# Three blocks of an expert stage: the second job's expert made fixed, 15 weight places instead of 12, 18 unrolled jobs instead of 8, and the gather of tokens cut in two

## The chip, the cores and the metric

The kernel runs on one NeuronCore of a Trainium2 chip. The metric is the device time of one execution in microseconds (us), taken as the median of several runs. The profile is one execution more; its times are counted from the start of its span.

## The reference, cut to what matters

Two models stand one behind the other, on 256 tokens of width 1024. The first (attention, gated feed-forward, a per-layer embedding; two layers) is untouched here. The second has two layers of a hybrid mixer (windowed attention beside a short convolution) and then this mixture of experts:

```
group  = argmax(x @ w_rg + b_rg)                  # 4 groups of 8 experts
e1, e2 = the two best of the group's 8 experts    # x @ w_re + b_re
y      = sum over e in (e1, e2) of gate_e * ((silu(x @ w_gate[e]) * (x @ w_up[e])) @ w_down[e])
```

There are 32 experts with matrices 1024x512, 1024x512 and 512x1024 in float32, so 2 MiB each and 6 MiB (6.29 MB) for an expert. The 256 tokens give 512 pairs of token and expert. On the fixed inputs the reference's routing gives every expert of the first layer at least one token (expert 0 has 16) and leaves one of the second layer empty, expert 21 (expert 0 has 9); no expert has more than 48.

## The kernel before, in words

**Jobs.** The expert stage (`moe(l)`, once for each of two layers) sorts the 512 pairs by expert into 512 slots. A job is one expert with a window of 64 slots (`W`). Expert e gets ceil(count/64) jobs, and each of the first `FORCED` = 10 experts at least one, even when it is empty. A small table `tab` holds the expert and first slot of each job and the number `more` of jobs that go through a hardware loop. Job 0 is always expert 0, so that its weights need no table. The table is made by a chain of small VectorE and TensorE instructions (`route`, lines 2433 to 2521, and lines 1703 to 1729) and copied out of PSUM on line 1073. The SyncE queue, which issues all weight loads, waits for it on line 698 before it reads the number of job 1's expert.

**Weights.** A job's weights are six halves of 1 MiB: gate 0, 1, up 0, 1, down 0, 1. There are twelve places of 1 MiB: six in `raw` and six in `spare`, a second name for the memory of `parts` (the rounded weights of the dense stages). In the first `FIXED` = 8 jobs, which are written out (unrolled), jobs 0, 2, 4 and 6 go to `spare` and the odd ones to `raw`. Later jobs use `raw` alone, in a hardware loop. Before a place is loaded again SyncE waits (line 658 to 672) until TensorE has counted its last use in the semaphore `used`. Loads are issued in one fixed order, two halves (2 MiB) at a time.

**Work of a job.** TensorE runs step j: turn the gate product of job j-1 (line 1788, 4 transposes), gate half 0 of job j (line 1779), turn the up product, gate half 1, turn the result of job j-2 (line 1798), up half 0 and 1, and the down product of job j-1 (line 1809). ScalarE and VectorE copy between them. The token window of a job, `xw`, is a copy that ScalarE makes out of `xsT`, the gathered and turned tokens (line 1091).

**Ahead of the jobs.** TensorE gathers all 512 slots by matmuls with a 0/1 matrix `sel` (128 x 512 for each half of the tokens): 8 column blocks x 2 token halves x 2 parts (high and low) = 32 matmuls of 128x512 on line 1742. Their stationary operand is `xsp`, read with a stride of 8 elements (`view(xsp[:, i, :], D * t + k, [[KC, P]])`). `sel` is written by VectorE on lines 2520 and 2521. ScalarE and VectorE scale the eight banks into `xsT` (lines 1079, 2540) and ScalarE copies job 0's window (line 1084). After job 0's four products TensorE turns `sel` for the later way back (line 1753) and sums the gates of each slot (line 1759), and only then step 1 begins. Short matmuls without use ("spin", line 1687) fill TensorE's waits during routing.

**After the jobs.** The results are turned back and added into the tokens (line 1870); in the first of the two layers the next layer's dense stage follows, whose loads stand behind the last job's in the SyncE queue.

Of the kernel before, what the change touches and what calls it, by code (L numbers as in the profile page):

```python
# [20 lines left out]
F32 = mybir.dt.float32  # L21
# [6 lines left out]
P = 128  # L28
# [22 lines left out]
JOBS = NE + NS // W  # L51
FIXED = 8
IN_PARTS = (0, 2, 4, 6)
FORCED = 10
# [11 lines left out]
C_ID, C_TRI, C_I512, C_I32, C_I4, C_VALID, C_COS, C_SIN, C_SEL, C_W = 0, 128, 256, 768, 800, 804, 805, 821, 837, 897  # L66
# [7 lines left out]
def build(nc, A, out):  # L74
    ctx = ExitStack()
    with ctx:
# [10 lines left out]
        h = sb("h", [P, NT, D])  # L87
        xT = sb("xT", [P, 2, KC, S], F32R)
# [128 lines left out]
        gsel = qkf[:, 2560:3584].rearrange("p (t s) -> p t s", t=NT)  # L217
        rt = qkf[:, 0:2048]
        gtmp = qkf[:, 2048:2560]
        asg0 = rt[:, 1280:1376]  # L220

        def gather_bank(k):

            return pb[(0, 1, 4, 5, 6, 7, 2, 3)[k]]
# [14 lines left out]
        arrived = [arrived[0], arrived[1], arrived[0], arrived[2]]  # L239
        hi_done = {g: sem(f"hi_done{g}") for g in (0, 2)}  # L240
# [56 lines left out]
        LOADS0 = []  # L297
# [50 lines left out]

        add_proj(0, A["w_in_ab"][0], [(512 * c, 512, 512 * c) for c in (0, 1, 3, 4, 2, 5)])
# [9 lines left out]
        for l in range(2):  # L359
# [10 lines left out]
            LOADS0.append(list(loads))  # L370
            for i in range(0, RAW, 2):
                loads[i] += len(IN_PARTS)

# [24 lines left out]
        def job_home(l, j, q):  # L398

            q -= q % 2  # L400
            if isinstance(j, int) and j <= FIXED:
                job, i = piece(j, q)
                if job in IN_PARTS:
                    part = (SPL0[2 * l + 1] + i // 2) % SPL
                    return spare[:, 2 * part:2 * part + 2, :], arrived[2 * l][i], 16 * (LOADS0[l][i] + job // 2 + 1)
                if job < FIXED - 1 or j < FIXED:
                    place = (RAW0[2 * l + 1] + i) % RAW
                    return raw[:, place:place + 2, :], arrived[2 * l + 1][place], 16 * ((job + 1) // 2)
            place = (RAW0[2 * l + 1] + q - 2) % RAW
            return raw[:, place:place + 2, :], arrived[2 * l + 1][place], at(j, 16, -8 * FIXED + (0 if q < 2 else 16))  # L410

        def last_half(l):

            return arrived[2 * l + 1][(RAW0[2 * l + 1] + 5) % RAW]

        def consumed(job, i):

            if job == 0 and i < 4:
                return (1, 3, 3, 4)[i]
# [2318 lines left out]
```

## Time and profile before

| what | us |
|---|---|
| median of 3 runs | 1922.22 |
| lowest and highest | 1920.95, 1923.99 |
| profiled execution, its own time | 1919.76 |
| its span | 1917.9 |
| TensorE busy | 1813.6 (95%) |
| VectorE busy | 862.6 (45%) |
| ScalarE busy | 763.7 (40%) |
| first expert stage: table's first load to last down product | 852.84 to 1323.4 |
| second expert stage, the same | 1445.04 to 1899.0 |

The mean granted TensorE clock of the execution is 0.991 of full speed. A busy TensorE is not one at its peak, since the ends of matmuls are modelled: two stages that both show it as busy can have different paces, which is read from the distance of like instructions. Most fp32 matmuls appear as two records, and some records are missing. The DMA share of a stretch is that of 16 engines, and may read slightly over 1.

### The profile page before, as it was taken

To read this page: it belongs to the slowest core of one execution; us is meant where nothing else is said; L and a number is where in the kernel's file an instruction comes from. 1 tells how busy PE (TensorE), PEld (TensorE's weight loads), DVE (VectorE), ACT (ScalarE), POOL (GpSimd) and SP (SyncE) were. 2 spreads that over 40 slices of the span, in tenths; PEclk is the share of its full clock that TensorE was granted. 3 is DMA by queue.
4 is the path that set the end of the run, shared out by engine and by line. 5 is a ranking of instruction groups with operands and counts; after the bars stand their busy time and mean duration, and the time that the engine had idled before them with its cause. 6 is when DMAs were issued, how large, how long until landed. Compare 5 with 4: busy or idle time off the path is not lost.

```text
span 1917.9 us, 27918 instructions
## 1 busy us (share of the span) xinstructions
PE 1813.6 (95%) x10239; PEld 1174.3 (61%) x10239; DVE 862.6 (45%) x1641; ACT 763.7 (40%) x1396; POOL 74.8 (4%) x98
## 2 busy tenths in 40 slices
PE   8999999998999999999999999999999999999997
PEld 6779998885799988874333333335975333333334
DVE  4766566578766566872211111114784111111113
ACT  5564334556543345523333332334532333333333
POOL 3300000110000000010000000000010000000000
PEclk9999999998999999999999999999999999999999
DMA  9546554551355545159999999998438999999995
GB/s 324 205 143 198 184 190 154 185 177 34 120 185 189 185 155 186 45 208 409 428 400 428 428 429 428 429 428 337 136 132 343 429 409 428 427 431 427 429 429 221
DMA packets 127696, 549.14 MB, mean 286 GB/s; under 512 B 7711, under 2 KB 67449, under 8 KB 103161
## 3 DMA queue, kind: packets, MB, share of 16 engines
q1 hardware_dynamic: 124200, 539.51, 71.4%
q0 software_dynamic: 3088, 8.10, 1.3%
q8 instruction: 59, 0.97, 0.2%
q10 hardware_dynamic: 320, 0.34, 0.1%
q14 instruction: 29, 0.23, 0.0%
HBM read 546.81 MB, written 1.11 MB: 286 GB/s over the span
## 4 chain that ended last, share of the span: by engine, by line
PE 65%; DMA 24%; DVE 6%; ACT 2%; issue 1%; POOL 1%; SPq 0%; POOLq 0%; DVEq 0%; ACTq 0%
PE pb L1242 27%; DMA raw<-in_w_expert_down 24%; PE pb L1809 12%; PE pb L1779 8%; PE pb L1537 6%; PE pb L1788 1%; PE pb L1371 1%; PE pb L1471 1%; PE pb L1798 1%; DVE parts L1963 1%; PE pb L1394 1%; PE pb L1348 1%; POOL rms L792 1%; PE pb L1742 1%; PE pb L1254 1%
## 5 line engine op out<-in xcount | busy, mean ns | idle before, releaser
L1779 PE MATMUL pb<-raw,xw 128*64 128x512 f32 x1760 | 415.0, 603 | 19.8 <-DMA raw<-in_w_expert_gate 19.7
L1963 DVE TENSOR_TENSOR parts<-raw,parts 128x2048 fp32r<-128x2048 f32 (+1 forms) x138 | 307.1, 2231 | 108.3 <-ACT parts L812 105.3
L812 ACT ACTIVATE parts<-raw 128x2048 fp32r<-128x2048 f32 (+1 forms) x138 | 256.6, 1867 | 209.7 <-PE pb L1242 153.2
L1242 PE MATMUL pb<-xT,parts 128*128 128x256 f32 (+1 forms) x2712 | 333.3, 283 | 0.0
L1242 PEld LDWEIGHTS pb<-xT,parts 128*128 128x128 f32 (+1 forms) x2712 | 329.2, 191 | 4.7 <-issue 2.9
L2555 DVE TENSOR_TENSOR qk<-qk,pb 128x256 f32<-128x256 f32 x126 | 53.1, 421 | 605.1 <-ACT qk L1101 605.0
L1242 PE MATMUL pb<-parts,xT 128*128 128x512 f32 (+1 forms) x1200 | 272.1, 385 | 2.9 <-DVE xT L1974 1.5
L1242 PEld LDWEIGHTS pb<-parts,xT 128*128 128x128 f32 x1200 | 217.9, 189 | 49.0 <-issue 4.3
L1779 PEld LDWEIGHTS pb<-raw,xw 128*64 128x64 f32 x1760 | 111.9, 136 | 204.2 <-issue 167.9
L1809 PE MATMUL pb<-raw,qk 128*64 128x512 f32 x880 | 201.0, 596 | 35.1 <-DMA raw<-in_w_expert_down 35.1
L1809 PEld LDWEIGHTS pb<-raw,qk 128*64 128x64 f32 x880 | 67.6, 136 | 162.9 <-issue 162.7
L1096 ACT ACTIVATE qk<-pb 128x512 f32<-128x512 f32 x126 | 74.9, 594 | 172.9 <-PE pb L1779 172.9
L1113 ACT ACTIVATE qk<-pb 128x512 f32<-128x512 f32 x126 | 68.4, 595 | 159.3 <-PE pb L1809 159.3
L1788 PEld LDWEIGHTS pb<-cst,qk 128*128 128x128 f32 x504 | 70.2, 209 | 98.5 <-issue 97.8
L1537 PE MATMUL pb<-parts,hidT 128*128 128x512 f32 x528 | 124.3, 391 | 3.1 <-DVE hidT L2197 3.1
L1537 PEld LDWEIGHTS pb<-parts,hidT 128*128 128x128 f32 x528 | 97.7, 188 | 23.3 <-DVE hidT L2197 3.9
L1101 ACT ACTIVATE qk<-pb 128x256 f32<-128x256 f32 x126 | 48.8, 388 | 146.4 <-PE pb L1788 146.2
L2573 DVE TENSOR_TENSOR work<-work,pb 128x256 f32 x126 | 53.0, 422 | 93.6 <-ACT work L1120 92.9
L1788 PE MATMUL pb<-cst,qk 128*128 128x128 f32 x504 | 93.7, 309 | 0.5 <-DVE rms L2583 0.5
L1120 ACT ACTIVATE work<-pb 128x256 f32 x126 | 48.4, 386 | 113.9 <-PE pb L1798 111.0
L1798 PEld LDWEIGHTS pb<-cst,qk 128*128 128x128 f32 x504 | 54.2, 141 | 48.1 <-issue 47.9
L1798 PE MATMUL pb<-cst,qk 128*128 128x128 f32 x504 | 68.6, 279 | 0.0
(322 smaller groups left out, 1490.3 us busy)
## 6 DMA issues: line engine op xcount, KB each, us to landing
raw<-in_w_expert_gate SPq DMA_DIRECT2D x55, 2048.0 KB, 10.0
raw<-in_w_expert_up SPq DMA_DIRECT2D x55, 2048.0 KB, 10.4
raw<-in_w_expert_down SPq DMA_DIRECT2D x53, 2048.0 KB, 10.7
raw<-in_w_ffn_gate SPq DMA_DIRECT2D x22, 1024.0 KB, 5.4
raw<-in_w_ffn_up SPq DMA_DIRECT2D x22, 1024.0 KB, 5.4
raw<-in_w_ffn_down SPq DMA_DIRECT2D x22, 1024.0 KB, 5.0
raw<-in_w_in SPq DMA_DIRECT2D x16, 1024.0 KB, 5.3
spare<-in_w_expert_gate SPq DMA_DIRECT2D x8, 2048.0 KB, 11.3
```

Source lines behind the costliest of these rows:

```text
L812: nc.scalar.activation(parts[:, (SPL0[seg] + k) % SPL, 0, 0:kk * nn], raw[:, place, 0:kk * nn], ACT.Copy).then_inc(hi_done[seg], 1)
L1096: nc.scalar.activation(dst, pb[bank][:], ACT.Copy).then_inc(done[l], 1)
L1113: nc.scalar.activation(ys[:, 512 * c:512 * (c + 1)], pb[4 + c][:], ACT.Copy).then_inc(ys_done[l], 1)
L1242: ins = mm(out_ap, b if flip else a, a if flip else b, start=first and n == 0, stop=last and n == 2)
L1537: ins = mm(pb[2 * c + t][:], hidT[:, j, i, P * t:P * (t + 1)], w[p][:, j, 512 * c:512 * (c + 1)], start=(q == 1 and j == 0 and n == 0), st ...
L1779: ins = mm(pb[m][rows, :], xw[:, 4 * hf + k, :], w[:, k, :], start=(hf == 0 and k < 2), stop=(hf == 1 and k >= 2))
L1788: ins = nc.tensor.transpose(pb[2 + m][:, P * q:P * (q + 1)], view(src, q, [[DE // P, P]]), ident)
L1798: ins = nc.tensor.transpose(pb[6 + b][:, P * q:P * (q + 1)], ys[:, 512 * b + P * q:512 * b + P * (q + 1)], ident)
L1809: ins = mm(pb[4 + c][W * k:W * (k + 1), :], ehj[:, 2 * hf + k, :], w[:, k, 512 * c:512 * (c + 1)], start=(hf == 0), stop=(hf == 1))
L1963: v.tensor_tensor(two[:, 1, :], raw[:, place, 0:kk * nn], two[:, 0, :].bitcast(F32), ALU.subtract)\
L2555: v.tensor_tensor(d, d, pb[2 + m][:].rearrange("p (k i s) -> p k i s", k=4, i=2)[:, :, 1, :], ALU.add)\
L2573: v.tensor_tensor(d, d, pb[6 + b][:].rearrange("p (k i s) -> p k i s", k=4, i=2)[:, :, 1, :], ALU.add)\
```

## The change

The 33rd bin takes what expert 0 has beyond 64 tokens, so that expert 0 always has exactly one job in front, and job 1 is always expert 1. Its weights are then loaded without the table. Three places of 1 MiB are added (`extra`, a second name for the memory of `xT` and `xs`, free once the router has read it). A planner (`plan`) hands out 15 places to the halves of jobs 0 to 18, singly where a pair would wait longer, and goes back to the six of `raw` for the last ones. `FIXED` goes from 8 to 18, `FORCED` from 10 to 20. The gather first makes 128 slots (`EARLY`) for jobs 0 and 1 in two banks, and the other 384 in two groups behind job 0's products and inside step 1. The turning of `sel` and the gate sums move into step 12 (`GATES_AT`). The first waits for the `raw` places are those of the last rounding of each place, not of all.

```diff
-JOBS = NE + NS // W
-FIXED = 8
-IN_PARTS = (0, 2, 4, 6)
-FORCED = 10
+BINS = NE + 1
+JOBS = BINS + NS // W
+FIXED = 18
+EXTRA = 3
+FORCED = FIXED + 2
+EARLY = 2 * W
+GATES_AT = 12
...
+        with nc.sbuf_tensor("extra", [P, EXTRA, HALF], F32) as extra:
+            pass
...
+        def first_wait(l, kind, i):
+
+            seg, n = 2 * l, len(stream[2 * l])
+            if kind == "raw":
+                before = max(k for k in range(n) if stream[seg][k][2] == (RAW0[seg + 1] + i) % RAW)
+                return [(lo_done[seg], before + 1)]
+            if kind == "spare":
+                return [(used[seg], n - SPL + i // 2 + 1)]
+            return [(rt_ready, l + 1), (sq_done, 2 * (7 + 2 * l) + 2)]
...
+            order = [(0, 0), (0, 2), (1, 0), (1, 2), (0, 4), (1, 4)]
+            for job in range(2, FIXED + 1):
+                order += [(job, 0), (job, 2)] + ([(job - 1, 4)] if job > 2 else [])
+            for job, i in order:
+                first = use_of(job, i)
+                if first >= LAST_FIXED - 6:
+                    put(job, i, [("raw", first % RAW), ("raw", first % RAW + 1)])
+                    continue
+                free = [p for p in places if p[0] != "raw" or first < LAST_FIXED - 12]
+                pair = min((p for p in pairs if p[0] in free), key=lambda p: max(rank[p[0]], rank[p[1]]))
+                single = sorted(free, key=lambda p: rank[p])[:2]
+                if max(rank[p] for p in pair) <= rank[single[1]] + (2 if job >= 7 else 0):
+                    put(job, i, pair)
+                else:
+                    put(job, i, single[:1])
+                    put(job, i + 1, single[1:])
...
@@ SyncE
-                sp.wait_ge(lo_done[2 * l], len(stream[2 * l]))
-                gate_up_of(0, 0)
-                down_of(1, 0)
+                units = PLAN[l][0]
+                early = [unit for unit in units if unit[0] < 2]
+                for unit in early:
+                    load_fixed(l, unit, unit[0])
                 sp.wait_ge(tab_done, l + 1)
...
@@ ScalarE
+                def gathered(half):
+
+                    for k in (4 * half, 4 * half + 2):
+                        act.wait_ge(ga_ready, (KC + 2) * l + 2 + k + 1)
+                        nc.scalar.activation(xsT[:, k, EARLY:NS], gather_bank(k)[:, 0:NS - EARLY], ACT.Copy,
+                                             scale=gperm[:, l, k:k + 1]).then_inc(xsT_a, 1)
...
@@ TensorE
-                spin(10)
+                mm(count, over, ones[0:1, :], start=True, stop=False)
+                mm(pos, ones[0:1, :], view(over, 0, [[0, 2], [1, BINS]]), start=True, stop=False)
+                pe.wait_ge(xsT_v, 9 * l + 1)
+                for b in (4, 5):
+                    mm(pb[b][:], ones[0:1, :], xsT[0:1, :, NS:NSP], start=True, stop=False)
+                spin(8)
...
-                spin(3)
-                pe.wait_ge(tab_done, l + 1)
+                for t in range(NT):
+                    for i in range(2):
...
+                        for k in range(KC):
+                            ins = mm(early_bank(k), tokens(i, t, k), sel[:, t, 0:EARLY],
+                                     start=False, stop=(t == 1 and i == 1 and k % 4 == 3))
...
+                def gathered(half):
+
+                    pe.wait_ge(sel_done, 6 * l + 4)
+                    for k in range(4 * half, 4 * half + 4):
...
+                        for t in range(NT):
+                            for i in range(2):
+                                ins = mm(gather_bank(k)[:, 0:NS - EARLY], tokens(i, t, k), sel[:, t, EARLY:NS],
                                          start=(t == 0 and i == 0), stop=(t == 1 and i == 1))
...
+                    if fixed == 1:
+                        gathered(1)
+                        pe.wait_ge(xsT_a, 4 * l + 3)
+                        pe.wait_ge(xsT_v, 9 * l + 8)
...
-                first = gate_up(0)
-                pe.wait_ge(xsT_a, 5 * l + 3)
-                products(0, *first[0])
-                products(0, *first[2], done=0)
-                pe.wait_ge(xw_ready[l], 1)
-                products(0, *first[1], done=2)
-                products(0, *first[3])
-                gates_turned()
-                pe.wait_ge(gct_done, 3 * l + 3)
+                for n, one in enumerate(gate_up(0)):
+                    if n < 2:
+                        pe.wait_ge(xsT_v, 9 * l + n + 2)
+                    products(0, *one)
+                gathered(0)
                 for j in range(1, FIXED):
                     step(j)
+                    if j == GATES_AT:
+                        gates_turned()
...
@@ VectorE
+                def chosen(t, cols):
+
+                    link(v.tensor_scalar(sel[:, t, cols], i512[:, cols], sl[0][:, t:t + 1], None, ALU.is_equal))
+                    v.scalar_tensor_tensor(sel[:, t, cols], i512[:, cols], sl[1][:, t:t + 1], sel[:, t, cols].bitcast(F32),
+                                           ALU.is_equal, ALU.add).then_inc(sel_done, 1)
...
+                for half in range(2):
+                    x, g = early(half)
+                    dve.wait_ge(ga_ready, (KC + 2) * l + half + 1)
+                    v.tensor_tensor(xw[:, 4 * half:4 * half + 4, :], x[:, :, 0:W], g[:, :, 0:W], ALU.mult).then_inc(xsT_v, 1)
```

## Rows read from the trace of the kernel before

**Rows 1.** The page: ScalarE's copies of gate and up products, two for each job.

```profile
L1096 ACT ACTIVATE qk<-pb 128x512 f32<-128x512 f32 x126 | 74.9, 594 | 172.9 <-PE pb L1779 172.9
```

**Rows 2.** The chain that ended last, end of the first expert stage (start, us, what).

```profile
978.28 10.92 DMA raw<-in_w_expert_down
989.33 3.67 PE pb L1809 x16
...
1297.70 3.65 PE pb L1809 x16
```

**Rows 3.** TensorE's timeline, first transposes of steps 2, 8 and 10, first stage.

```profile
886.10 0.75 PE L1788 MATMUL pb<-cst,qk 128*128 128x128 f32 x4
...
964.90 0.75 PE L1788 MATMUL pb<-cst,qk 128*128 128x128 f32 x4
...
992.92 0.75 PE L1788 MATMUL pb<-cst,qk 128*128 128x128 f32 x4
```

**Rows 4.** The same, steps 1, 2 and 10 of the second stage.

```profile
1464.15 0.75 PE L1788 MATMUL pb<-cst,qk 128*128 128x128 f32 x4 [0.25 <-DVE rms L2583]
...
1476.11 0.75 PE L1788 MATMUL pb<-cst,qk 128*128 128x128 f32 x4
...
1583.30 0.75 PE L1788 MATMUL pb<-cst,qk 128*128 128x128 f32 x4
```

**Rows 5.** Stretches: length; PE, PEld, DVE, ACT, POOL busy; clock; DMA share; GB/s.

```profile
900.00:920.00 20.00, 20.00 (x100) 8.06 (x102) 4.89 (x12) 7.19 (x17) 0.00 (x0) 1.00 1.01 428
...
966.00:980.00 14.00, 13.94 (x70) 5.43 (x68) 2.87 (x7) 4.92 (x12) 0.00 (x0) 1.00 0.87 325
```

**Rows 6.** SyncE's queue: the third early load, then the first load behind the table.

```profile
834.32 0.33 SPq L672 DMA_DIRECT2D spare<-in_w_expert_down  x1
852.84 0.35 SPq L672 DMA_DIRECT2D raw<-in_w_expert_gate  x1
```

**Rows 7.** VectorE's timeline: last op of the job columns; the longer one for `sel`.

```profile
850.30 0.25 DVE L2512 SCALAR_TENSOR_TENSOR qk<-cst,qk 32x40 f32<-32x40 f32 x1
...
851.62 0.75 DVE L2521 SCALAR_TENSOR_TENSOR hidT<-cst,qk,hidT 128x512 fp32r<-128x512 f32 x1
```

**Rows 8.** TensorE's timeline: job 0, turned `sel`, gate sums, step 1 (first stage).

```profile
862.48 7.09 PE L1779 MATMUL pb<-spare,xw 128*64 128x512 f32 x32
...
869.50 1.09 PE L1753 MATMUL pb<-cst,hidT 128*128 128x128 f32 x8
870.42 1.84 PE L1759 MATMUL pb<-ones,qk 128*128 128x1 f32 x16
872.52 0.98 PE L1788 MATMUL pb<-cst,qk 128*128 128x128 f32 x4 [0.26 <-DVE rms L2583]
```

**Rows 9.** The same of the second stage: gather, job 0.

```profile
1445.77 8.41 PE L1742 MATMUL pb<-hidT,xsp 128*128 128x512 f32 x32
1454.10 7.09 PE L1779 MATMUL pb<-spare,xw 128*64 128x512 f32 x32
```

**Rows 10.** Stretches of dense 256-column, dense 512-column and gather matmuls (columns as Rows 5).

```profile
776.00:780.00 4.00, 4.00 (x36) 4.00 (x35) 3.90 (x11) 1.79 (x9) 0.00 (x0) 1.00 0.48 187
...
822.00:830.00 8.00, 8.00 (x36) 6.38 (x34) 6.27 (x9) 0.00 (x1) 1.27 (x2) 1.00 0.61 229
...
857.00:861.00 4.00, 4.00 (x18) 4.00 (x18) 2.73 (x5) 1.69 (x3) 0.00 (x0) 1.00 1.03 434
```

**Rows 11.** Weight loads by line: gather (strided), router (not strided); min/median/max ns.

```profile
L1742 PEld LDWEIGHTS pb<-hidT,xsp x32: 317/332/342, 853.2 to 861.9; 128*128 128x128 f32 x32
...
L1700 PEld LDWEIGHTS pb<-hidT,xT x32: 186/192/192, 833.9 to 840.5; 128*128 128x128 f32 x32
```

**Rows 12.** Stretches of 1 us with a lowered clock (columns as Rows 5).

```profile
855.00:856.00 1.00, 1.00 (x4) 0.82 (x3) 0.00 (x0) 0.00 (x0) 0.00 (x0) 0.61 1.06 426
...
874.00:875.00 1.00, 1.00 (x4) 0.23 (x2) 0.37 (x1) 0.00 (x0) 0.00 (x0) 0.50 0.95 393
```

**Rows 13.** VectorE's timeline: the last rounding of a dense weight ahead of the first stage.

```profile
821.71 2.29 DVE L1963 TENSOR_TENSOR parts<-raw,parts 128x2048 fp32r<-128x2048 f32 x1 [0.62 <-ACT parts L812]
```

More of the change, by code:

```diff
@@ L296, in build @@
         loads = [0] * RAW
-        LOADS0 = []
         def add(seg, src, k, n):
@@ new lines, in plan, with put @@
+        def plan(l):
+            places = [("raw", i) for i in range(RAW)] + [("spare", i) for i in range(2 * SPL)] + [("extra", i) for i in range(EXTRA)]
+            pairs = [[places[i], places[i + 1]] for i in (0, 2, 4, 6, 8, 10, 12)]
+            rank = {p: n - len(places) for n, p in enumerate(places)}
+            raw_loads = [0] * RAW
+            units, homes = [], {}
+            def put(job, i, where):
+                kind, x = where[0]
+                if kind == "raw":
+                    x = (RAW0[2 * l + 1] + x) % RAW
+                if kind == "spare":
+                    x = 2 * ((SPL0[2 * l + 1] + x // 2) % SPL) + x % 2
+                buffer, there, count = {"raw": (raw, arrived[2 * l + 1], raw_loads), "spare": (spare, arrived[2 * l], loads),
+                                        "extra": (extra, extra_in, extra_loads)}[kind]
+                count[x] += 1
+                waits = []
+                for n, p in enumerate(where):
+                    for there_sem, at_least in ([(used[2 * l + 1], rank[p] + 1)] if rank[p] >= 0 else first_wait(l, *p)):
+                        if not any(one is there_sem and n0 >= at_least for one, n0 in waits):
+                            waits = [w for w in waits if w[0] is not there_sem] + [(there_sem, at_least)]
+                    homes[job, i + n] = (buffer[:, x + n, :], there[x], 16 * count[x])
+                    rank[p] = use_of(job, i + n)
+                units.append((job, i, len(where), buffer[:, x:x + len(where), :], there[x], waits))
+            order = [(0, 0), (0, 2), (1, 0), (1, 2), (0, 4), (1, 4)]
[14 more added lines that the diff above has]
+                    put(job, i + 1, single[1:])
+            return units, homes, raw_loads
@@ L369, in build @@
             SPL0[seg + 1] = (SPL0[seg] + len(stream[seg])) % SPL
-            LOADS0.append(list(loads))
-            for i in range(0, RAW, 2):
-                loads[i] += len(IN_PARTS)
+            PLAN.append(plan(l))
         def at(j, per_job, more):
@@ L1135, in step @@
                         window(j)
+                    if not later and j:
+                        gathered(0)
                     if later:
@@ L1752, in gates_turned @@
+                    ins.then_inc(gct_ready, 1)
+                    pe.wait_ge(yadd_done[l], at(GATES_AT, 2, -1))
+                    for c in range(4):
+                        b = pb[6 + c // 2]
                         for t in range(NT):
@@ L2596, in step @@
                         low_slots(0)
+                    if not later and j:
+                        gathered(0)
                     if later or j:
@@ L2599, in step @@
                         hidden(j, 1)
-                    else:
-                        combine()
+                    if not later and j:
+                        gathered(1)
                     if later:
```

287 lines of the change are left out of this document (151 added, 136 removed).

## The prediction

> **What bounds the kernel now.** I read the chain of waits first. In the first expert stage it is TensorE's own work up to 978, and from there each step ends on a landing of down weights: 21 steps between 989.33 and 1297.70, so 14.68 us a step [rows 2]. The timeline of TensorE shows the other pace: from step 2 at 886.10 to step 8 at 964.90, (964.90 - 886.10) / 6 = 13.13 us a step, with no wait [rows 3]. The stretches tell what sets each: the DMA share is 1.01 and 428 GB/s in both [rows 5], and a job's 6.29 MB at 428 GB/s are 14.7 us. So the weights are the slower side by 14.69 - 13.13 = 1.55 us a job (I take 14.69 from here on), and TensorE runs at its own pace only while it eats what was stored ahead. 126 copies of gate and up products are 63 jobs [rows 1], 32 in the first stage and 31 in the second.
>
> Why does the store end at step 8? Jobs 0 to 8 have twelve places; from job 9 on only six are used, and its first load waits until step 8 has used the gate weights. After that step the chain hangs on the loads: step 8 to step 10 takes 992.92 - 964.90 = 28.0 us, and then 14.69 each. In 966 to 980 the DMA share sags to 0.87 [rows 5]: the queue waits for TensorE there, 14 x (428 - 325) / 428 = 3.4 us lost.
>
> **The main term.** With 18 unrolled jobs and 15 places the same hand-over stands at step 18. If TensorE keeps its pace up to there, ten more steps cost 13.13 instead of 14.69: 15.55 us a stage, 31.1 us for both. The end of a stage is then the start of step 18 plus 28.0 plus the loads' pace, as before, so every us by which step 18 comes late goes off the gain, one for one.
>
> **What moves TensorE's start.** First stage, step by step.
> - Job columns end at 850.55 [rows 7]. The new small operation on the slots is like its neighbours, 0.2; product and sum 0.6 as now; `sel` for 128 columns instead of 512 takes two operations that are shorter than the 0.75 of the row, about 0.3 each. The early gather can start at about 851.9, and its later parts find their operands.
> - The early gather has 32 matmuls as the whole one has now, each with a quarter of the columns. What does one cost? A count in a stretch includes the two that its edges cut. In the gather's stretch PEld is busy 4.00 of 4.00 us and 16 matmuls pass, 0.25 each; dense matmuls of the same 512 columns pass at 8 / 34 = 0.235 with PEld busy 6.38 of 8; those with 256 columns pass at 4 / 34 = 0.12, PEld full again [rows 10]. A weight load of the gather takes 332 ns against 192 for one whose operand has no stride [rows 11]; 192 goes with a pace of 0.12, that is 0.07 less, and 332 less 0.07 is 0.26. So the strided weight loads fill the gather already, and fewer columns free nothing. Bounds: 32 x 0.12 = 3.8 us below, 32 x 0.25 = 8.0 above; I take 8.0, since its row is of the very same load. End 859.9, and job 0's first product starts there instead of at 862.48 [rows 8]: -2.5. Second stage: from 1444.3 to 1452.3 against 1454.10 [rows 9]: -1.8.
> - The late gathers are 32 matmuls of 384 columns: 16 behind job 0, 16 inside step 1. Bounds 32 x 0.176 (three quarters of 0.235) = 5.6 and 32 x 0.25 = 8.0; by the same row +8.0.
> - Turned `sel` and gate sums leave that place: from 869.50 to 872.52, -3.0 [rows 8]. They come back in step 12 with 0.95 + 1.84 = +2.8; its copies run on VectorE beside two turns and two products.
> - The clock. In the first stage the granted clock stood at 0.5 in 874 to 875 [rows 12], right after the 128x1 sums of line 1759, and step 1 took 886.10 - 872.52 = 13.6 against 1476.11 - 1464.15 = 12.0 in the second [rows 3, 4, 8]. Without those sums ahead of it this 1.6 goes: -1.6, first stage only.
>
> Sum: first stage -2.5 + 8.0 - 3.0 + 2.8 - 1.6 = +3.7, second -1.8 + 8.0 - 3.0 + 2.8 = +6.0; together 9.7 late. But the clock also has new occasions to drop: it was low at the start of the gather, too [rows 12], the early gather's matmuls fill less than half of TensorE's time, and the sums in step 12 are again a sparse stretch. Bounds: nothing, or 1.6 for the step behind the sums and 2.4 for job 0 (in 855 to 856 the clock was still 0.61 [rows 12], some 5 us after the columns' end at 850.55 from where TensorE was dense; half of 5 us is lost at half speed), 4.0 a stage. I allow 1.6 a stage, 3.2 in all, what one such drop was seen to cost.
>
> **Sum:** 31.1 - 9.7 - 3.2 = 18.2 us. The profiled execution has 1919.76, so 1901.6; the median of the runs shown is 2.5 above it, 1922.2, so **1904**.
>
> **The loads' side must allow this.** Jobs 0 and 1 are twelve halves. Two `raw` pairs are free before the last rounding, which ends at 824.0 [rows 13], the third there, the last `spare` pair at 834.3 as now [rows 6]. From 824 eight halves at 14.69 / 6 = 2.45 are 19.6 us, so all are in by 846, ahead of the table at 852.84 [rows 6]. Behind the table 30 jobs remain instead of 31, one job less to carry: 14.7 us. Three halves go to `extra` at once (7.3 us, to about 861.5), then the queue waits for job 0's first product, about 1.7, and again while the two late gathers free no place, 2 each; waits for both places of a pair in jobs 4 to 7 may cost 2.5. That is 8 us idle where the queue now loses 3.4 and more, I put it at 5. So the loads alone allow 14.7 + 5 - 8 = 12 us in this stage, as TensorE does with 15.55 - 3.7 = 11.9. Neither side can gain much without the other.
>
> **Edits costed at nothing.** Two one-row matmuls of 512 columns and two small ones take the place of two spins ahead of the counts: +1.2 us of TensorE's time in a gap of 1.6. The 33rd bin widens small VectorE operations by one column. Scaling job 0's window: the first half runs under the gather's last four matmuls, the second under the first product. Evacuating the late banks: ScalarE and VectorE are busy 7.2 and 4.9 of 20 us in such steps [rows 5]; if they were late, step 1's down product would wait, 0.6 for each bank. More and smaller loads: 0.35 us of SyncE's time each against 2.4 us of transport.
>
> **A rule against my largest choice.** By the Trainium skill, "TensorE: Matmul & The Clock Gate", section "LDWEIGHTS (loading the stationary operand)", a load takes the time of its columns, 107 ns for 128, whatever else it is; both gathers would then be cheap, and that is rival A. The trace disagrees with it for this operand (332 ns in rows 11). The skill's "SBUF - State Buffer", section "Door 1: The DMA port swizzle", says that reads of fp32 strided by more than four elements pay a penalty; the stride here is eight, and the 332 against 192 ns agree.
>
> **The rivals.**
> - A, the gathers go by columns. Early 3.8, so job 0 starts at 856.4 and 1448.8; late 5.6. Then TensorE is 2.3 early in the first stage and level in the second, and 33 would come off; the loads' side, with some 4 us idle a stage, allows 30. Time 1892. For it: other 128-wide loads let 256 columns pass at 0.12; against it: PEld full at 0.25 here [rows 10].
> - B, the clock stays low after the sparse gather and drops again in step 12: 4.0 a stage, or 8.7 with all of job 0's 7.1 us doubled [rows 8]. Gain 31.1 - 9.7 - 8.0 = 13.4 down to 4.0, time 1909 to 1918.
> - C, slower. The unrolled steps 8 to 17 are new code, 20 in both stages, and need their instructions fetched through the same saturated DMA engines. Price: the excess of a step over 13.13, twenty times. The gain is 20 x (14.69 - s) - 12.9, nothing at s = 14.04 and a loss over 3.8 us from s = 14.23; at 14.69 the time is 1922.2 + 12.9 = 1935. Against it: steps 2 to 7 are unrolled code too, and ran at 13.13 with the DMA share at 1.01 [rows 3, 5].
> - D, it doesn't do what it says: an empty expert among 10 to 19 would now get a job, 14.7 us more, and the time would be 1919. The reference's routing leaves only expert 21 empty, so this is nearly excluded.
>
> **Chances.** Forecast (gain 14 to 24) 0.55, A 0.20, B 0.17, C 0.04, D or another wait that eats the gain 0.04. A measurement of this kernel tells about 0.2% from no change, 3.8 us. Faster by more 0.92, within 0.03, slower 0.05. The range takes in A with 3 us below it and B but for its worst end: 1889 to 1914.
>
> **What would show it.** In the changed kernel: job 0's first product at about 860 and 1452 with 32 early gather matmuls over 8 us (A: 4 us); a late gather of 4.0 us each (A: 2.8); steps 2 to 17 at 13.13, and down weights ending steps only from step 19 on; step 12 longer by 2.8; 63 jobs. The forecast is wrong if loads end waits before step 18, if the gathers pass at their columns' pace, or if the clock row stands at 0.5 behind 862.

## The result and the profile after

The changed kernel takes **1906.58 us** (median of 4 runs, 1904.11 to 1907.87) against 1921.83 for the kernel before (median of 4 runs beside them). The ratio is 0.9917, 95% interval 0.990 to 0.9935: 15.3 us faster, so 0.8%, and clear of the scatter. Run again on another chip it took 1906.41 (5 runs; ratio 0.9922, interval 0.9909 to 0.9936). The profiled execution took 1907.87 against 1919.76, so the sum below has to explain 11.9 us; medians and profiles differ here by some 3 us, which is the scatter of single executions.

The page first (the chain by engine of the kernel before, then of the changed kernel, and the copies that count the jobs):

```profile
PE 65%; DMA 24%; DVE 6%; ACT 2%; issue 1%; POOL 1%; SPq 0%; POOLq 0%; DVEq 0%; ACTq 0%
```

```profile
PE 74%; DMA 16%; DVE 6%; ACT 1%; issue 1%; POOL 1%; SPq 0%; POOLq 0%; DVEq 0%; ACTq 0%
...
L1159 ACT ACTIVATE qk<-pb 128x512 f32<-128x512 f32 x126 | 74.9, 594 | 196.6 <-PE pb L1871 196.6
```

Still 126 copies, so 63 jobs, as in [rows 1]. Landings of weights were 24% of the chain before and are 16% now. TensorE's waits in the first expert stage (us in total, times, longest), for down weights in the kernel before, then in the changed kernel:

```profile
PE pb L1809 <- DMA raw<-in_w_expert_down: 18.0, 22, 1.3
```

```profile
PE pb L1900 <- DMA raw<-in_w_expert_down: 10.1, 13, 0.8
PE pb L1871 <- DMA raw<-in_w_expert_gate: 6.7, 12, 1.5
```

Of 22 waits for down weights 13 are left. The first of them is in step 18, where it was in step 9 before, so nine steps no longer end on a landing. TensorE's timeline at the hand-over: the down product of step 17, step 18's first transposes and down product, the same of step 19:

```profile
1098.69 3.60 PE L1900 MATMUL pb<-extra,qk 128*64 128x512 f32 x16
1102.23 0.75 PE L1879 MATMUL pb<-cst,qk 128*128 128x128 f32 x4
...
1112.74 3.65 PE L1900 MATMUL pb<-raw,qk 128*64 128x512 f32 x16 [0.74 <-DMA raw<-in_w_expert_down]
1116.32 0.75 PE L1879 MATMUL pb<-cst,qk 128*128 128x128 f32 x4
...
1127.41 3.65 PE L1900 MATMUL pb<-raw,qk 128*64 128x512 f32 x16 [0.78 <-DMA raw<-in_w_expert_down]
```

Step 18 starts at 1102.23, and from its down product on each one waits for a landing, 1127.41 - 1112.74 = 14.67 apart. Now the start of the stage, where [rows 6 to 8] stood before (TensorE's timeline):

```profile
841.14 1.93 PE L1778 MATMUL pb<-qkv,ones 1*128 1x512 f32 x4
...
843.00 5.41 PE L1754 MATMUL pb<-cst,ones 128*128 128x256 f32 x16
...
848.33 0.62 PE L1783 MATMUL pb<-ones,qk 128*33 128x128 f32 x4
...
853.25 7.95 PE L1817 MATMUL pb<-hidT,xsp 128*128 128x128 f32 x32 [1.13 <-DVE hidT L2625]
861.13 8.26 PE L1871 MATMUL pb<-raw,xw 128*64 128x512 f32 x32
869.33 4.21 PE L1833 MATMUL pb<-hidT,xsp 128*128 128x384 f32 x16
...
881.78 4.19 PE L1833 MATMUL pb<-hidT,xsp 128*128 128x384 f32 x16
```

The same in the second stage:

```profile
1425.80 2.78 PE L1778 MATMUL pb<-qkv,ones 1*128 1x512 f32 x4
1428.52 6.20 PE L1754 MATMUL pb<-cst,ones 128*128 128x256 f32 x16
...
1439.56 7.94 PE L1817 MATMUL pb<-hidT,xsp 128*128 128x128 f32 x32 [1.12 <-DVE hidT L2625]
1447.43 8.66 PE L1871 MATMUL pb<-raw,xw 128*64 128x512 f32 x32
```

The gathers and steps look as forecast. What doesn't is the block ahead: the eight spins of line 1754, 3.65 us at full clock, take 5.41 and 6.20, so that in the first stage the count sums (line 1783) start at 848.33, though VectorE had delivered the assignment at 846.55. The stretches say why (columns as in [rows 5]; the last but two is the granted clock):

```profile
840.00:842.00 2.00, 2.00 (x12) 1.32 (x12) 1.11 (x6) 1.22 (x2) 0.70 (x1) 1.00 0.96 410
842.00:844.00 2.00, 2.00 (x6) 1.01 (x5) 1.69 (x10) 1.09 (x2) 0.00 (x0) 0.76 1.01 434
844.00:846.00 2.00, 2.00 (x6) 1.64 (x5) 1.76 (x8) 0.00 (x0) 0.00 (x0) 0.50 0.59 250
846.00:848.00 2.00, 2.00 (x9) 1.69 (x9) 1.75 (x5) 0.20 (x1) 0.00 (x0) 0.88 0.02 8
...
854.00:856.00 2.00, 2.00 (x10) 2.00 (x10) 0.98 (x1) 0.00 (x0) 0.00 (x0) 0.50 0.63 131
```

The clock is at 1.00, 2.4 GHz, up to 842 and at 0.50, 1.2 GHz, in 844 to 846: it fell during or right behind the two one-row matmuls of 512 columns, and the spins behind them ran at half speed. It is at 0.50 again in the early gather.

### The profile page after: what moved, and what is told of

It reads as the page before. It is cut to its first block, busy times and chain, and to the rows that moved or that the text cites. A ratio compares the mean times of both kernels' runs of the same rounds, so it can differ in the third digit from the quotient of the medians.

```text
span 1906.0 us, 27293 instructions
## 1 busy us (share of the span) xinstructions
PE 1827.6 (96%) x10299; PEld 1186.9 (62%) x10299; DVE 867.2 (45%) x1659; ACT 762.0 (40%) x1392; POOL 75.0 (4%) x98
## 4 chain that ended last, share of the span: by engine, by line
PE 74%; DMA 16%; DVE 6%; ACT 1%; issue 1%; POOL 1%; SPq 0%; POOLq 0%; DVEq 0%; ACTq 0%
PE pb L1309 27%; DMA raw<-in_w_expert_down 16%; PE pb L1871 14%; PE pb L1900 11%; PE pb L1604 6%; PE pb L1879 2%; PE pb L1889 2%; PE pb L1438 1%; PE pb L1538 1%; PE pb L1415 1%; DVE parts L2064 1%; PE pb L1461 1%; PE pb L1833 1%; POOL rms L852 1%; PE pb L1817 1%
## 5 line engine op out<-in xcount | busy, mean ns | idle before, releaser
L1871 PE MATMUL pb<-raw,xw 128*64 128x512 f32 x1360 | 322.4, 606 | 12.3 <-DMA raw<-in_w_expert_gate 12.3
L1871 PEld LDWEIGHTS pb<-raw,xw 128*64 128x64 f32 x1360 | 87.1, 137 | 156.8 <-issue 132.4
L1900 PE MATMUL pb<-raw,qk 128*64 128x512 f32 x624 | 142.8, 596 | 19.6 <-DMA raw<-in_w_expert_down 19.6
L1900 PEld LDWEIGHTS pb<-raw,qk 128*64 128x64 f32 x624 | 47.0, 136 | 108.9 <-issue 108.6
L1871 PE MATMUL pb<-spare,xw 128*64 128x512 f32 x464 | 109.2, 601 | 0.0
L1879 PE MATMUL pb<-cst,qk 128*128 128x128 f32 x504 | 93.0, 308 | 0.0
```

What stands on the lines that cost most here:

```text
L1871: ins = mm(pb[m][rows, :], xw[:, 4 * hf + k, :], w[:, k, :], start=(hf == 0 and k < 2), stop=(hf == 1 and k >= 2))
L1879: ins = nc.tensor.transpose(pb[2 + m][:, P * q:P * (q + 1)], view(src, q, [[DE // P, P]]), ident)
L1900: ins = mm(pb[4 + c][W * k:W * (k + 1), :], ehj[:, 2 * hf + k, :], w[:, k, 512 * c:512 * (c + 1)], start=(hf == 0), stop=(hf == 1))
```

## The experiments

Edits are against the changed kernel unless said otherwise. Experiments 1 to 4 share a chip, so do 5 to 8 and 9 to 11. Ratios are to the kernel before, run beside them.

**1. One row or 128 rows.** The matmuls that clear the early gather's banks multiply ones with a row of zeros. Here they read all 128 rows of the same zeros.

```diff
-                    mm(pb[b][:], ones[0:1, :], xsT[0:1, :, NS:NSP], start=True, stop=False)
+                    mm(pb[b][:], ones[:], xsT[:, :, NS:NSP], start=True, stop=False)
```

> The two matmuls that clear the early gather's banks (128x512 zeros) read 128 rows instead of one; nothing else differs from the changed kernel. Theory: a matmul that uses one row of the array lets the clock fall, and the eight spins behind it then run at the low clock, so the counts start late. Then here the granted clock stays at 1.00 in 842 to 848, the eight spins take 3.65 us instead of 5.41, the counts start at about 846.8 instead of 848.33 (as before the change) and the early gather at about 851.9; second stage 3.3 us earlier likewise; the run is 3 to 6 us faster than the changed kernel, about 1901 to 1904 us. Rival (the clock falls because TensorE is waiting or works on small matmuls ahead of this, whatever these two read): the clock row and the start of the counts stay as they were, the time stays at 1906 to 1908 us. In both, the early gather keeps its 8 us, since weight loads set it.

Measured: 1904.09 us (ratio 0.991, interval 0.9889 to 0.9932). TensorE's timeline and the stretches of the first stage:

```profile
842.49 1.98 PE L1778 MATMUL pb<-qkv,ones 128*128 128x512 f32 x4
844.31 3.62 PE L1754 MATMUL pb<-cst,ones 128*128 128x256 f32 x16
```

```profile
842.00:844.00 2.00, 2.00 (x8) 1.09 (x7) 1.71 (x10) 1.95 (x2) 0.01 (x1) 1.00 1.01 434
844.00:846.00 2.00, 2.00 (x10) 1.58 (x9) 1.76 (x9) 0.35 (x2) 0.00 (x0) 1.00 0.96 410
846.00:848.00 2.00, 2.00 (x11) 1.48 (x11) 1.76 (x9) 0.09 (x1) 0.00 (x0) 1.00 0.28 111
```

The clock stays at 1.00 up to the counts and the spins take 3.62 in both stages. In the six profiles with the one-row form and eight spins behind it (the changed kernel and experiments 3 and 5 to 8) they took 5.32 to 6.62 us, twelve times out of twelve. The matmuls themselves take the same 1.9 to 2.0 us in both forms while the clock is up. The absolute times that I expected for the first stage were not met, since this execution came to the block 1.3 us later (842.49 against 841.14 for line 1778); the second stage's gather came 3.3 us earlier, as expected (1436.23 against 1439.56). From line 1778 to step 1's down product it is 886.20 - 842.49 = 43.7 us, and 885.90 - 841.14 = 44.8 in the changed kernel; in the second stage 1469.50 - 1425.47 = 44.0 against 1472.59 - 1425.80 = 46.8. So 1.1 and 2.8 us come back. In time it is about 2.3 us between the ratios 0.991 and 0.9922: the mechanism is shown in the two stages of one profile; that the whole kernel is faster isn't, since the intervals overlap. Job 0 stays slow (8.57 us against 7.09): the clock falls anyway at 853.

**2. Fewer spins behind the one-row matmuls.**

```diff
-                spin(8)
+                spin(3)
```

> The eight spins behind the two one-row matmuls become three; the one-row matmuls stay. Theory: the counts are late because TensorE's queue still holds spins, run at the low clock, when the assignment is ready (846.55). With five spins less (5 x 0.68 = 3.4 us at the low clock, 2.3 at the high one) the queue is empty by about 845.5, and the counts start at 846.6 to 847.0 instead of 848.33, early gather at 851.6 to 852.2, second stage 3 us earlier; the clock is low in both stages from the one-row matmuls on, and job 0 may take 8 to 9 us again. Time about 3 to 5 us below the changed kernel. Rival (the lateness comes from something else, for instance the zero sums waiting for VectorE): the counts start at 848.3 as before. A second rival: fewer spins leave the clock at the low level for longer, the chain of small matmuls behind the counts gets slower by 1 to 2 us and takes the gain back.

Measured once: 1903.82 us. The clock is down as before, yet the queue is empty in time:

```profile
842.98 2.93 PE L1754 MATMUL pb<-cst,ones 128*128 128x256 f32 x6
846.51 0.62 PE L1783 MATMUL pb<-ones,qk 128*33 128x128 f32 x4 [0.60 <-DVE qk L2583]
...
851.89 7.94 PE L1817 MATMUL pb<-hidT,xsp 128*128 128x128 f32 x32 [1.00 <-DVE hidT L2625]
```

Counts at 846.51 instead of 848.33, gather at 851.89 instead of 853.25, which is where the prediction had put it. Of the 1.8 us 1.4 arrive at the gather: behind the earlier counts TensorE waits for VectorE twice (0.30 and 0.16 us), where the changed kernel didn't. The second rival has a part in it: behind the fewer spins the chain of the second stage ran at the low clock. From line 1778 to the early gather it is 1435.78 - 1424.29 = 11.5 us there, against 13.8 in the changed kernel and 10.8 in experiment 1, so three spins give 2.3 us back and the low clock keeps some 0.7. A single run doesn't tell what the whole kernel gains. So the lateness is spins left in TensorE's queue; the clock decides how many us they are.

**3. The stride of the weight loads.** The gathers read 128 features in a block instead of every eighth; the features of the gathered tokens then stand in another order, so something else is computed.

```diff
-                    return view(xsp[:, i, :], D * t + k, [[KC, P]])
+                    return xsp[:, i, D * t + P * k:D * t + P * (k + 1)]
```

> Leaves something else computed: both gathers read the token matrix in contiguous blocks of 128 features instead of every eighth feature, so that the features of the gathered tokens stand in another order; shapes, number and columns of all matmuls are the same. Theory: the gathers are bound by weight loads that read with a stride of eight elements, 0.25 us each. Without the stride a load takes 192 ns instead of 332 and passes at 0.12 to 0.13: the early gather takes about 4 us instead of 7.95, each late gather of 16 takes 16 x 0.176 = 2.8 us instead of 4.2, so step 2 starts 4 + 1.4 + 1.4 = 6.8 us earlier in both stages, and if the loads allow it the time is 8 to 13.6 us below the changed kernel. Rival (the 0.25 is the fixed cost of a load of fp32 that is rounded on the way, or of switching between banks): the early gather still takes 7.9 us, and the time stays within 1 us.

Measured once: 1902.45 us, where 8 to 13.6 us below the changed kernel were expected. Weight loads of the first late gather (busy us, mean ns of one), the changed kernel first, then this one:

```profile
L1833 PEld LDWEIGHTS pb<-hidT,xsp 128*128 128x128 f32 x16 | 3.9, 338 | 0.8 <-DVE qk L2636 0.8
```

```profile
L1833 PEld LDWEIGHTS pb<-hidT,xsp 128*128 128x128 f32 x16 | 2.7, 188 | 0.8 <-issue 0.8
```

A load takes 188 ns instead of 338, and a late gather 3.05 us instead of 4.21: bound by strided weight loads, as said. By the Trainium skill, "TensorE: Matmul & The Clock Gate", section "LDWEIGHTS (loading the stationary operand)", a load takes the time of its columns; the same 128 columns took 188 and 338 ns here, and the stride was the only difference, so the trace disagrees with the rule for this operand. The early gather was a half miss: 6.30 and 7.09 us, not 4. The clock was 0.65 in 854 to 856 and 0.50 behind it, and job 0 took 9.51 instead of 8.26. So the low clock took much of what the loads gave. From the start of the early gather to step 1's down product it is 883.64 - 853.71 = 29.9 us against 885.90 - 853.25 = 32.6, a gain of 2.7 where 6.8 was expected: 1.65 of the early gather and 2.3 of the late ones, less 1.25 in job 0.

**4. The whole gather back.** All 512 slots ahead of job 0 again, 32 matmuls of 512 columns, with the old banks, copies, windows and spins; the unrolled jobs, the three more places and the gate sums in step 12 stay. Its core:

```diff
-                            for k in range(KC):
-                                ins = mm(early_bank(k), tokens(i, t, k), sel[:, t, 0:EARLY],
...
+                            for k in range(4 * group, 4 * group + 4):
+                                ins = mm(gather_bank(k)[:], tokens(i, t, k), sel[:, t, :],
...
-                for b in (4, 5):
-                    mm(pb[b][:], ones[0:1, :], xsT[0:1, :, NS:NSP], start=True, stop=False)
-                spin(8)
+                spin(10)
```

> The changed kernel with the old whole gather: all 512 slots in one go ahead of job 0 (32 matmuls of 512 columns), with the old banks, copies and windows and the old ten spins; the eighteen unrolled jobs, the three more weight places and the gate sums in step 12 stay. Theory: splitting the gather in two is itself a loss, because each of the 64 matmuls of the two parts needs a strided weight load of 0.25 us, where the whole gather needs 32; and the clearing matmuls and spins made the table late. By the sum of steps: step 2 starts at about 881.5 instead of 889.5 in the first stage and some 10 us earlier in the second, and every us of it comes off the end: 17 to 18 us below the changed kernel, about 1889 us (1885 to 1894). Rival (the loads' side binds before: the first places come free later, since job 0's first product is 2 us later and the loads of the later jobs end the waits from an earlier step on): the first down product that waits for a landing is at step 13 to 17 instead of 19, and the gain is only 5 to 12 us. A second rival (the early gather is worth what it costs): the time is 1906 to 1910 us.

Measured: **1896.80 us** (5 runs, 1895.45 to 1898.90; ratio 0.9877, interval 0.986 to 0.9894). So the cut of the gather, with the clearing matmuls that came with it, is itself a loss, of 0.9922 - 0.9877 = 0.0045, 8.6 us; the two intervals don't touch. How much of it is the clearing and its clock isn't separated: experiment 1, which has the cut but not the fall behind the clearing matmuls, stands 7.3 us above this kernel on the same chip, with intervals that just overlap. And 8.6 is half of what I expected. TensorE's timeline:

```profile
852.11 9.14 PE L1812 MATMUL pb<-hidT,xsp 128*128 128x512 f32 x32
861.18 7.09 PE L1851 MATMUL pb<-raw,xw 128*64 128x512 f32 x32
869.67 0.75 PE L1860 MATMUL pb<-cst,qk 128*128 128x128 f32 x4 [1.41 <-ACT xw L1152]
...
881.63 0.75 PE L1860 MATMUL pb<-cst,qk 128*128 128x128 f32 x4
...
1088.43 3.65 PE L1851 MATMUL pb<-spare,xw 128*64 128x512 f32 x16 [0.87 <-DMA spare<-in_w_expert_up]
1093.27 3.65 PE L1881 MATMUL pb<-extra,qk 128*64 128x512 f32 x16 [1.19 <-DMA extra<-in_w_expert_down]
```

Job 0 starts no later than in the changed kernel (861.18 against 861.13) though it has four times the gathered columns behind it, and runs at full clock. Step 2 starts at 881.63, as expected (881.5), 7.9 us ahead of the changed kernel. Then two waits, 0.87 and 1.19, meet TensorE in step 17 (which starts at 1081.25), for halves of the store: 2.1 us go to the loads in this stage and 1.8 in the second, and the lead at the first stage's last down products is 5.7 us. That is the first rival as it was put: first waits in steps 13 to 17, a gain of 5 to 12. The queue's own gap shows in the stretches:

```profile
862.00:864.00 2.00, 2.00 (x12) 0.72 (x10) 1.93 (x4) 1.01 (x3) 0.00 (x0) 1.00 0.02 8
864.00:866.00 2.00, 2.00 (x12) 0.62 (x10) 0.05 (x1) 0.00 (x0) 0.00 (x0) 1.00 0.71 201
866.00:868.00 2.00, 2.00 (x12) 0.53 (x8) 0.00 (x0) 0.60 (x1) 0.00 (x0) 1.00 1.17 377
868.00:870.00 2.00, 0.59 (x4) 0.33 (x3) 0.00 (x0) 1.23 (x2) 0.00 (x0) 1.00 0.68 274
```

With all places full or waiting for job 0's first products, the queue moves 8, 201, 377 and 274 GB/s where 428 would pass: 2 x (4 x 428 - 860) / 428 = 4.0 us lost. How TensorE's start gets to the end of the stage is seen in longer stretches, of the changed kernel, then of this one:

```profile
854.00:894.00 40.00, 40.00 (x172) 23.70 (x174) 13.65 (x26) 9.00 (x18) 0.00 (x0) 0.88 0.88 328
894.00:954.00 60.00, 60.00 (x296) 23.47 (x294) 11.05 (x27) 20.65 (x45) 0.00 (x0) 1.00 1.00 415
954.00:1100.00 146.00, 146.00 (x726) 58.75 (x724) 28.36 (x69) 49.62 (x110) 0.00 (x0) 1.00 1.01 428
```

```profile
854.00:894.00 40.00, 38.59 (x179) 18.58 (x179) 10.64 (x21) 12.63 (x25) 0.00 (x0) 0.99 0.91 370
894.00:954.00 60.00, 60.00 (x296) 23.80 (x294) 11.67 (x29) 20.97 (x48) 0.00 (x0) 1.00 1.01 426
```

Against 428 GB/s the changed kernel's queue loses 9.35 + 1.8 = 11.2 us between 854 and 954, this one 5.4 + 0.3 = 5.7; behind that both move 427 to 428. The difference, 5.5, is about the lead of 5.7. So in this stage of both kernels the queue is full from 954 on, and a late TensorE costs time by freeing the first places late: the first load of up weights that goes into `spare` again is issued at 889.60 in the changed kernel and at 881.74 here.

**5. The changed kernel once more**, no edit, as the base of experiments 6 to 8.

> The changed kernel itself once more, unedited, so that the edits of this group are compared on one chip, and to learn how much of its loss in the table chain repeats. Theory (the one-row matmuls of 512 columns let the clock fall): the eight spins behind them take over 5 us again in both stages and the counts start late; time 15 us below the kernel before, within 2. Rival (the fall was chance): in at least one stage the spins take 3.6 us and the counts are on time, as in the run with 128 rows.

Measured: 1906.41 us (ratio 0.9922, interval 0.9909 to 0.9936). The spins took 6.23 and 5.41 us: the loss repeats.

**6. Eight unrolled jobs.** The new places, the cut gather and the fixed second job stay.

```diff
-FIXED = 18
+FIXED = 8
-GATES_AT = 12
+GATES_AT = 6
```

> Eight unrolled jobs instead of eighteen, so that the three more places serve no further job; gate sums in step 6; all else as in the changed kernel. Theory (the gain is the number of steps that TensorE makes at 13.13 us instead of 14.69, less its lateness of some 6 us a stage): steps from 10 on come at 14.69, down weights end waits from step 9 on, and the time is 22 to 27 us above the changed kernel, so 7 to 12 us above the kernel before. Rival (the gain comes from somewhere else: the job that runs no more, the earlier first loads, the shorter start): at most 5 us above the changed kernel.

Measured: 1938.19 us (ratio 1.0089, interval 1.0074 to 1.0105), 31.8 us above experiment 5. TensorE's waits are those of the kernel before:

```profile
PE pb L1900 <- DMA raw<-in_w_expert_down: 17.9, 22, 1.3
PE pb L1871 <- DMA raw<-in_w_expert_gate: 9.9, 21, 0.5
```

31.8 is the prediction's main term, 31.1, almost to the number. The two profiled executions are 30.0 us apart (1937.62 - 1907.66), so the agreement is good to some 2 us. My 22 to 27 was too low, and what I wrote ahead of the run has no term for the difference. It also shows the price of all the rest: without the unrolled steps the change is a loss of 1938.19 - 1920.73 = 17.5 us, where the prediction's terms had 9.7 + 3.2 = 12.9.

**7. Eighteen unrolled jobs, the old twelve places.**

```diff
-            places = [("raw", i) for i in range(RAW)] + [("spare", i) for i in range(2 * SPL)] + [("extra", i) for i in range(EXTRA)]
-            pairs = [[places[i], places[i + 1]] for i in (0, 2, 4, 6, 8, 10, 12)]
+            places = [("raw", i) for i in range(RAW)] + [("spare", i) for i in range(2 * SPL)]
+            pairs = [[places[i], places[i + 1]] for i in (0, 2, 4, 6, 8, 10)]
```

> The eighteen unrolled jobs stay, but the three more weight places aren't used: the jobs have the old twelve. Theory (places and unrolled steps count only together: a place is a half job, 2.45 us of transport, stored ahead, and three of them are 7.3 us a stage): the loads fall behind TensorE before step 18, waits for landings begin around step 12 to 14, and the time is 10 to 15 us above the changed kernel, near or some us below the kernel before. Rival (the loads have slack, the places are not what carries the unrolled steps): the same time as the changed kernel within 2 us, first waits at step 18 or 19.

Measured: 1924.18 us (10 runs; ratio 1.0018, interval 1.0008 to 1.0028), 17.8 above experiment 5. The first waits for landings, in steps 11 and 12 instead of 18:

```profile
1020.17 3.65 PE L1900 MATMUL pb<-spare,qk 128*64 128x512 f32 x16 [0.43 <-DMA spare<-in_w_expert_down]
...
1034.85 3.65 PE L1900 MATMUL pb<-spare,qk 128*64 128x512 f32 x16 [0.79 <-DMA spare<-in_w_expert_down]
```

The loads have no slack. Three places are 3 x 2.45 x 2 = 14.7 us of transport in two stages, and 17.8 us were lost: a bit more than they hold. Places and unrolled steps pay only together.

**8. Twenty-four unrolled jobs, fifteen places.** FORCED keeps its 20, with the least value of `more` set to 1.

```diff
-FIXED = 18
+FIXED = 24
-FORCED = FIXED + 2
+FORCED = 20
```

> Twenty-four unrolled jobs instead of eighteen, with the same fifteen places. Theory (after step 18 the store is empty in any case: from step 2 to 18 TensorE eats 16 x 1.55 = 25 us of transport more than comes in, and the loads' own pace of 14.69 sets every later step): the same time as the changed kernel within 1.5 us; single landings end waits from step 18 to 20 on, and the later steps come every 14.69 us. Rival (the hand-over behind step 18 to the six places is the limit, so each further unrolled step brings its 1.55 us too): up to 6 x 1.55 x 2 = 18 us below the changed kernel.

Measured: 1910.18 us (4 runs, 1905.88 to 1912.36; ratio 0.994, interval 0.9921 to 0.9959), 3.8 above experiment 5, with intervals that overlap; within 1.5 was expected. No gain from six more unrolled jobs: at step 18 the store is empty, and the hand-over is no limit of its own.

**9. The whole gather once more**, the kernel of experiment 4, unedited, as the base of 10 and 11.

> The whole gather in the changed kernel once more, unedited: it is the version that beat both, and the two edits of this group are compared with it on one chip. Theory: 22 to 25 us below the kernel before, 8 to 10 us below the changed kernel's ratio (0.992); step 2 of the first stage starts at 880 to 882, and three waits for loads ahead of step 19 (an up weight, a down weight in the extra place, 2.1 us together) come again in each stage. Rival (a lucky profile): the waits come elsewhere or not at all, the time is within 3 us of the changed kernel.

Measured: 1897.88 us (ratio 0.9876, interval 0.9859 to 0.9892), the same waits in step 17 (0.9 and 1.2 us, in the second stage 0.8 and 1.2). The gain over the changed kernel repeats.

**10. The whole gather with seventeen unrolled jobs** (against experiment 9).

```diff
-FIXED = 18
+FIXED = 17
```

> The whole gather with seventeen unrolled jobs instead of eighteen, nothing else. Theory (with the whole gather TensorE is so early that the loads' side sets the end: the last unrolled steps wait for landings, 2.1 us a stage): the seventeenth place of the hand-over costs nothing or little, since the last step of TensorE's own pace was spent in those waits; the time is within 1 us of the whole gather with eighteen, at most 2 us above. Rival (TensorE still sets the end, each unrolled step is worth its 1.55 us): 3.1 us above, two stages of 1.55, with no waits ahead of step 18.

Measured: 1896.27 us (ratio 0.9865, interval 0.9849 to 0.9882): not the 3.1 us more that TensorE's side would cost, rather 1.6 less, within the scatter. The waits ahead of the hand-over are gone in the first stage and 0.5 us in the second; the hand-over itself, now in step 17, has a wait of 1.97 us in the first stage. With the whole gather the loads set the end of the stages. Whether the changed kernel could do with seventeen as well wasn't run.

**11. The small one-row matmuls behind the spins** (against experiment 9).

```diff
                 mm(count, over, ones[0:1, :], start=True, stop=False)
                 mm(pos, ones[0:1, :], view(over, 0, [[0, 2], [1, BINS]]), start=True, stop=False)
-                spin(10)
```

with `spin(10)` now ahead of the two.

> The whole gather with the two small one-row matmuls (33x128 and 128x66 columns) that start the count and position sums behind the ten spins instead of ahead of them; nothing else. Theory (small one-row matmuls can tip the clock as well: with the whole gather it fell right behind them in one of two stages, at 841): the clock stays at 1.00 until the counts in both stages, the spins take 4.6 us, the counts start at about 845.5 to 846.7 and not behind late spins; 0 to 2 us below the whole gather. Rival (that fall had to do with the waits of the router's sums before, not with one-row operands): the clock falls in one or both stages as before, the spins take over 5.5 us there, and the time is the same within 1 us.

Measured: 1897.45 us (ratio 0.9875, interval 0.9858 to 0.9891), no difference. TensorE's timeline of experiment 9, then of this one:

```profile
840.67 0.40 PE L1768 MATMUL pb<-ones,cst 1*33 1x128 f32 x2
...
841.37 6.27 PE L1748 MATMUL pb<-cst,ones 128*128 128x256 f32 x20
```

```profile
840.03 4.56 PE L1748 MATMUL pb<-cst,ones 128*128 128x256 f32 x20
```

In the three profiles of the whole gather with the small one-row matmuls ahead (experiments 4, 9 and 10), ten spins took 6.27 us in five stages of six and 4.58 in one; here 4.56 in both, as before the change. So the small ones tip the clock too, if not always. It gains nothing here, since the loads set the end. In both stages the clock fell in the count chain instead (0.50 from 850 and from 1430 on), and the gather took 9.58 and 9.50 us, against 9.26 and 9.14 in experiment 9.

## Why the prediction was right, and where it wasn't

It said 1904, faster, by a gain of 18.2 us against the profiled execution; 11.9 was profiled. Where these 6.3 us went can be read off the starts of the steps. Step 2 began at 889.49 against 886.10, 3.4 us late, where the terms ahead of it had given 3.7 - 2.8 + 1.6 = 2.5; in the second stage, with the 7.85 us that the changed kernel is ahead there, at 1476.18 + 7.85 = 1484.03 against 1476.11, 7.9 late where they had given 6.0 - 2.8 + 1.6 = 4.8. That is 0.9 + 3.1 = 4.0. The way from step 18 to step 20 took 28.8 and 29.3 us instead of 28.0 and 28.4: 1.7. One late wait for gate weights in the first stage, 1.5 us long where 0.5 is usual, cost 0.9. Step 12 gave 0.2 back. 18.2 - 4.0 - 1.7 - 0.9 + 0.2 = 11.8. Point by point:

- **The main term, 31.1 us, was right** but for that hand-over: steps of 13.13 us up to step 18, the loads' pace behind it. Down weights ended waits from step 18 on and not "only from step 19 on", which is the 1.7 above. Experiment 6 takes the term away and costs 31.8.
- **"The strided weight loads fill the gather already": right**, 7.95 and 7.94 us against 8.0, and the late ones 4.21 and 4.19 against 4.0 (0.8 us more in both stages together). Rival A is out, and experiment 3 shows the cause. (Its sum was 0.7 us off: 851.9 + 3.8 is 855.7 and 1444.3 + 3.8 is 1448.1, not 856.4 and 1448.8.)
- **"Edits costed at nothing" is the step that failed.** "Two one-row matmuls of 512 columns and two small ones: +1.2 us in a gap of 1.6" counted their time, and not what the clock does behind them. The eight spins grew from 3.65 to 5.41 and 6.20 us, and the early gathers, expected at 851.9 and 1444.3, began at 853.25 and 1439.56 + 7.85 = 1447.4: 1.4 and 3.1 us late, 4.5 together, which is all of the 4.0 above and a little more. Experiments 1 and 2 give 1.1 to 2.8 us a stage of it back, by the clock and by the queue.
- **The clock allowance, 3.2 us, was about right, but not its place.** Job 0 took 8.26 and 8.66 instead of 7.09, 2.7 together. Step 12, which I feared as much, took 2.7 us more as its rows foretold, without a fall.
- **The other rivals.** C: the new unrolled code ran at 13.13 from the first step. D: 63 jobs. B was half there: the clock was at 0.50 through the whole early gather. That costs the gather nothing that can be seen (0.248 us a matmul, [rows 10] had 0.25 at 1.00), but it slows job 0's first products. With it one of the prediction's own signs of being wrong came: the clock row was still low behind 862 (0.62 in 862 to 864).
- **"The loads' side must allow this"** held in kind, and "neither side can gain much without the other" is what experiments 7 and 10 show. It was put at 12 us a stage, with 8 us of the queue idle; the stretches of experiment 4 show 11.2 idle in the first stage. With that its sum is 14.7 + 5 - 11.2 = 8.5, and the changed kernel ended the first stage 8.0 us earlier. The whole gather, with 5.7 idle, gained 1920.73 x (1 - 0.9877) = 23.6 in two stages.
- **Not tested by itself:** the fixed second job with its earlier loads, one job less behind the table. Experiments 6 and 7 both keep it.

Of the four differences in the sum only the 0.2 went the other way, so no large one hid another. What I didn't see is that one part of the change works against the rest. The early gather was to start job 0 sooner by doing a quarter of the columns, and my own rows said that columns weren't what it waits for. I wrote down -2.5 and +8.0 us for the two parts, and yet no rival for the kernel without them; it is 8.6 us faster than the change.

## What to carry to other kernels

Before cutting a piece of TensorE's work into an urgent and a late part, find out whether it is bound by columns or by weight loads: if by loads, each part costs the whole. Where a stage has two sides (TensorE's pace and the loads'), undo each part of a change by itself, since one that hurts can hide behind another's gain, and add up what the queue loses, since a late engine frees its places late. And a filler that is to bridge a wait should be short enough to be over in time at half the clock.

## What the runs showed of the hardware

- Matmuls whose operands have one row take as long as with 128 rows (1.93 against 1.98 us for two of 512 columns), but the granted clock fell during or right behind them: eight spins took over 5.3 us in twelve stages of twelve, and 3.62 us, with the clock at 1.00, in both stages with 128 rows. With only two small ones, 5 of 6 stages fell; with these moved behind the spins, none of 2. Why experiment 1, which has the small ones ahead too, stayed up is open.
- A stationary operand read with a stride of eight fp32 elements loads in 338 ns, the same without the stride in 188 (late gather, clock 1.00). At clock 0.50 both come closer: the strided early gather keeps its 0.248 us a matmul, the unstrided one took 7.09 / 32 = 0.222 in the second stage, all of it at 0.50, where a late one at 1.00 took 3.05 / 16 = 0.19 with three times the columns.
- Three weight places of 1 MiB were worth 17.8 us in two stages, slightly more than the 14.7 us of transport that they hold.
